# Four quarter operations in place of one for the low part of each weight tile, on GpSimd

## The reference, cut to what matters

```python
x = x + 0.5 * SwiGLU(rmsnorm(x))                      # ffn1, inner width 2816
P = rmsnorm(x) @ w_in                                 # attention q/k/v | RWKV | gates
A = dilated attention, three groups of windows        # 8 heads of 64
R = RWKV-7 time mixing                                # 8 heads of 64
x = x + (sigmoid(gA) * (A @ w_branch_attn) + sigmoid(gR) * (R @ w_branch_rwkv)) @ w_out
x = x + 0.5 * SwiGLU(rmsnorm(x))                      # ffn2
```

## Time and profile before

| | us |
|---|---|
| median of 3 runs | 1869.22 |
| lowest and highest | 1863.80 and 1869.26 |
| the profiled execution's own time | 1864.62 |
| its span, first to last instruction | 1862.8 |
| mean granted TensorE clock | 0.982 of full speed |

### The profile page before, as it was taken

The page is one execution under the profiler, slowest core; times in us unless marked ns, Lnnn a source line. Parts: engine busy times, 40 slices in busy tenths (PEclk is TensorE's granted clock), DMA queues, the critical chain, the costliest instruction groups (busy, mean ns, idle before and its releaser), DMA issues.

```text
span 1862.8 us, 41273 instructions
## 1 busy us (share of the span) xinstructions
PE 1767.9 (95%) x17052; PEld 1680.8 (90%) x17052; DVE 763.9 (41%) x1110; ACT 610.5 (33%) x809; POOL 537.8 (29%) x210
## 2 busy tenths in 40 slices
PE   6999999997989999989999999999989999999999
PEld 5999999996879898987787989897889999999999
DVE  4333023323564645454475463627367333023320
ACT  4332122222423232332243443435224333123321
POOL 2333333442212121111122222223133434333332
PEclk9999999998999999999899999999999999999999
DMA  4334233332432234221154444435433333333343
GB/s 162 113 124 133 101 113 124 121 120 78 179 133 81 90 109 146 80 88 59 37 197 174 162 172 165 176 140 213 177 118 115 113 124 129 125 101 124 125 138 121
DMA packets 53111, 237.48 MB, mean 127 GB/s; under 512 B 7040, under 2 KB 7680, under 8 KB 51584
## 3 DMA queue, kind: packets, MB, share of 16 engines
q1 hardware_dynamic: 45120, 219.40, 34.2%
q10 hardware_dynamic: 7872, 16.37, 2.3%
HBM read 217.98 MB, written 71.76 MB: 156 GB/s over the span
## 4 chain that ended last, share of the span: by engine, by line
PE 55%; issue 24%; DVE 11%; POOL 5%; ACT 2%; DVEq 1%; ACTq 1%; POOLq 0%; PEldq 0%; DMA 0%; PEld 0%
PE ps L343 41%; POOL w_lo L330 5%; PE ps L789 3%; DVE qkv L1988 2%; DVE work L379 1%; DVE work L380 1%; PE ps L1847 1%; DVE qkv L1094 1%; ACT w_hi L325 1%; PE ps L1785 1%; DVEq L2039 1%; PE ps L1771 1%; DVE probs L383 0%; DVE xx L1135 0%; DVE qkv L1101 0%
## 5 line engine op out<-in xcount | busy, mean ns | idle before, releaser
L330 POOL TENSOR_TENSOR w_lo<-w_raw,w_hi 128x1024 fp32r<-128x1024 f32 (+1 forms) x202 | 532.0, 2634 | 1305.8 <-ACT w_hi L325 1305.7
L343 PE MATMUL ps<-h_hi,w_hi 128*128 128x288 f32 x2464 | 554.1, 307 | 25.8 <-DVE h_lo L464 11.2
L343 PE MATMUL ps<-h_hi,w_lo 128*128 128x288 f32 x2464 | 528.9, 296 | 0.0
L343 PE MATMUL ps<-h_lo,w_hi 128*128 128x288 f32 x2464 | 528.2, 296 | 0.0
L343 PEld LDWEIGHTS ps<-h_hi,w_hi 128*128 128x128 f32 x2464 | 398.8, 190 | 50.1 <-issue 20.6
L343 PEld LDWEIGHTS ps<-h_lo,w_hi 128*128 128x128 f32 x2464 | 398.3, 189 | 0.0
L343 PEld LDWEIGHTS ps<-h_hi,w_lo 128*128 128x128 f32 x2464 | 398.1, 189 | 0.0
L325 ACT ACTIVATE w_hi<-w_raw 128x1024 fp32r<-128x1024 f32 (+1 forms) x204 | 226.3, 1110 | 461.0 <-PE ps L343 443.9
L343 PE MATMUL ps<-g_hi,w_hi 128*128 128x288 f32 x704 | 151.4, 297 | 0.1
L343 PE MATMUL ps<-g_lo,w_hi 128*128 128x288 f32 x704 | 151.2, 296 | 0.0
L343 PE MATMUL ps<-g_hi,w_lo 128*128 128x288 f32 x704 | 151.2, 296 | 0.0
(11 more groups left out here) (364 smaller groups left out, 1919.4 us busy)
## 6 DMA issues: line engine op xcount, KB each, us to landing
w_raw<-in_w SPq DMA_DIRECT2D x172, 512.0 KB, 3.7
w_raw<-in_w SPq DMA_DIRECT2D x32, 704.0 KB, 4.1
kv<-in_kc SPq DMA_DIRECT2D x32, 576.0 KB, 6.1
kv<-in_vc SPq DMA_DIRECT2D x32, 576.0 KB, 7.6
cache_out<-in_cache SPq DMA_DIRECT2D x28, 576.0 KB
gates<-gate_out ACTq DMA_DIRECT2D x16, 288.0 KB, 2.3
cache_out<-in_cache SPq DMA_DIRECT2D x8, 480.0 KB
kvT<-qkv ACTq DMA_DIRECT2D x4, 864.0 KB, 7.1
```

Of the source, the lines that this page charges most:

```text
L330: nc.gpsimd.tensor_tensor(w_lo[par_][:, 0:words], w_raw[par_][:, 0:words], w_hi[par_][:, 0:words].bitcast(F32), ALU.subtract).then_inc(lo_ ...
L343: last = nc.tensor.matmul(ps[:, b + c, 0:HC], w[par_][:, wk], a[:, k, c * HC:(c + 1) * HC], start=(first and k == 0), stop=(end and k == n ...
```

## The change

`split_lo` issues four subtractions, each on a quarter of the tile's columns (256 of 1024, or 352 of 1408), instead of one. POOL waits once before the first and signals once, after the last. Nothing else is changed.

```diff
         def split_lo(pool, P, par_, words):
             pool.wait_ge(hi_done, 2 * P + par_ + 1)
-            nc.gpsimd.tensor_tensor(w_lo[par_][:, 0:words], w_raw[par_][:, 0:words],
-                                    w_hi[par_][:, 0:words].bitcast(F32), ALU.subtract).then_inc(lo_done, 1)
+            for i in range(4):
+                c = slice(words // 4 * i, words // 4 * (i + 1))
+                last = nc.gpsimd.tensor_tensor(w_lo[par_][:, c], w_raw[par_][:, c], w_hi[par_][:, c].bitcast(F32), ALU.subtract)
+            last.then_inc(lo_done, 1)
```

## The result

The kernel with four quarters takes **1853.41 us** in the median of 6 runs (1847.63 to 1856.85), the kernel before, run beside it, 1867.31 us in the median of its 6 (1863.8 to 1869.26). The ratio is 0.9925, with a 95% interval of 0.9907 to 0.9943. The profiled execution took 1854.38 us, 10.2 less than the one of before.

The account below looks back on a forecast made before the run. PE, busy 95% of the span, was taken as the bound, so gains come only from its 95 us idle. Costs of +4.6 and gains of -11.25 us gave -6.6, off the median: 1862.6 us, range 1856 to 1877.

Parts of the forecast that it names:

- DVE gets in between two pieces: At every quarter, a waiting DVE operation gets its turn after at most 0.6 to 0.7 us; POOL pays about 0.6.
- POOL doesn't let DVE in: Rival: the next quarter takes the inputs first, DVE waits 2.79 us instead of 2.39; up to +11.6 us, 1881; chance 0.20.
- The gains are hidden or given back: Rival: attention and merge gaps end with the next late thing, half the gain comes through; -1.0 us, 1868; chance 0.20.
- A short operation costs more than the line says: Rival: at 0.40 us per added operation, 38 even FFN units and seven tight units pay; +9.3 us, 1878.5; chance 0.10.
- The price, +4.6 us: Four first down units cost +1.6 us, waits at 15.02, 39.40 and 1447.05 +3.0; the 38 even units 0.
- Mix norm, -1.55 us: At 451.73, line 406 waits only for the first quarter, so PE's sum at 454.25 starts earlier: -1.55 us.
- Merge, -4.4 us: At the merge's end, `m_lo` no longer waits for whole low parts; PE starts about 1371.9 instead of 1376.26: -4.4 us.
- FFN2's norm, -0.4 us: Before 1436.30, four DVE operations each wait for a quarter; only 0.4 of PE's 1.31 us is gained.
- Attention, -4.9 us: In four periods line 1988 ends earlier and PE's waits of 0.28, 0.33 and 0.62 go: -4.9 us.
- RWKV, 0: In four periods PE is 1.4 us late for a low part but loses a 1.47 wait: 0, between -3 and +3.
- Idle time as a whole, -6.6 us: Sum of all terms over the kernel, +4.6 - 11.25 = -6.6 us, all from PE's idle time.
- From 1869.2 us: Starting time from which the -6.6 us was taken: the median of three runs of the kernel before, giving 1862.6.

Follow-up runs that it names:

- e3_longer: Kernel before with the low part whole, plus a short POOL operation of 120 columns into a scratch tile that carries the signal: 1875.0 us, ratio 1.0052.
- e4_half: Kernel before with the low part in two halves in every stage: 1853.1 us, ratio 0.9936.
- e5_rw4: Kernel before with quarters only in the mix norm and RWKV stages: 1862.8 us, ratio 0.9985.
- e6_at4: Kernel before with quarters only in the attention stage: 1859.8 us, ratio 0.9966.
- e7_mg4: Kernel before with quarters only in the merge and output projection: 1859.0 us, ratio 0.9966.
- e1_mid4: Kernel before with quarters in mix norm, RWKV, attention, merge and output projection, both FFNs whole: 1849.9 us, ratio 0.9909.
- e2_ffn4: Kernel before with quarters in both FFNs only, everything between them whole: 1871.7 us, ratio 1.0036.
- e10_tight4: Kernel before with quarters only at each FFN half's first two pairs of up units and first pair of down units: 1871.9 us, ratio 1.0050.
- e8_mid2: Kernel before with halves in all stages outside the FFNs, both FFNs whole: 1850.2 us, ratio 0.9919.
- e12_mix244: Kernel before with FFNs whole, halves in mix and RWKV, quarters in attention, merge and output projection: 1849.2 us, ratio 0.9914.
- e11_ffn8: Kernel before with eight pieces per low part in both FFNs, the middle whole: 1881.9 us, ratio 1.0097.

## Why the prediction was right in sign and wrong in size

The mechanism was right, and so was nearly every term in which a wait was read from the trace. Three things failed. The term for RWKV was put at 0, from one period read and multiplied by four; it is -1.8 us. TensorE's clock was put at nothing, without a reason; by the runs it gives about 3 us. And the forecast started from a median of three runs that lay high, 2 us of the 9.2 between forecast and result. The points in turn:

- **DVE gets in between two pieces** (the assumption on which all gains hung). Right. The merge's rows and the RWKV rows show it at seams with no wait and no signal, and e3_longer and e4_half show that it is the seams inside the low part that matter. The forecast's 0.6 to 0.7 us of waiting was too much: DVE operations take 1.12 to 1.18 in place of 0.76, and POOL pays (4.41 - 2.82) / 4 = 0.4 us for each that comes in, where 0.6 was taken.
- **POOL doesn't let DVE in** (slower, chance 0.20). Fell: its own mark, 1.3 against 2 us, is answered by 1118 ns for `m_lo`. The rule of the Trainium skill (GPSIMD Engine Reference, 2.1 Instruction dispatch) that was set beside it, that each of GpSimd's cores goes on with the next instruction when its own share is done, doesn't lead here to a POOL that holds on to its inputs.
- **The gains are hidden or given back** (0.20). Fell: e5 to e7 bring together what e1_mid4 does.
- **A short operation costs more than the line says** (0.10). Fell: 0.43 us for three added operations, 1.00 for seven (2.39 to 3.39 or 3.40), 0.143 each in both. The Trainium skill (GPSIMD Engine Reference, 3.1 Elementwise), from whose figures I had estimated 0.18 for three, doesn't agree with the trace.
- **The price, +4.6 us.** The places were right: four first down units at 0.39 to 0.49, 2.33 to 3.28 and 2.33 to 3.27 at 1447.05 and 39.40, and no wait in the even units. Waits on `w_lo` rise by 4.6 us in e2_ffn4 and in e10_tight4. In time this costs 6.6 and 7.1 us in medians when it stands alone; with the middle split too, the change is by the ratios 3.0 us (0.16%) above e1_mid4, by the medians 3.5, but from another group of runs. Between 3 and 7 the runs don't decide.
- **Mix norm, -1.55 us.** Right: the gap of 4.52 us is 2.90 now.
- **Merge, -4.4 us.** Right as idle time: 7.75 to 3.31. Measured alone (e7_mg4) it brings 5.5 us of idle time and 6.3 by the ratio; 4.4 of the 5.5 are this wait, the rest are waits of under 0.5 us elsewhere.
- **FFN2's norm, -0.4 us.** It is 1.31 to 0.72, so -0.6.
- **Attention, -4.9 us.** The three waits went as said, 1.23 us a period, but by another path: DVE gets ahead at the low part before, and the operation at line 1988 meets none. A period is 1.44 us shorter; the other 0.2 is in PE's busy time. e6_at4 has 6.2 us less idle time.
- **RWKV, 0.** This term failed. It put four waits of 1.4 us on `w_lo` against four of 1.47, from the reading of one period. PE's waits on the feature arrays (`qkv`) in the kernel before were in fact 4.4 us in three periods and 2.0 in the remaining one, the first in time:

```profile
PE ps L754 <- DVE qkv L1101: 4.4, 3, 1.5
...
PE ps L754 <- DVE qkv L1097: 2.0, 1, 2.0
```

  Both are gone from the list after (6.4 us), against three waits of 1.17 and 1.04 more at 519.43 (1.62 to 2.66 in e5_rw4): 4.6. That leaves -1.8 us.
- **Idle time as a whole, -6.6 us.** It is -10.1. Wait by wait in the change's own trace, with the forecast beside it: `w_lo` in the FFNs +4.6 (+4.6), mix norm -1.6 (-1.55), FFN2's norm -0.6 (-0.4), merge -4.4 (-4.4), attention -5.0 (-4.9), RWKV -1.8 (0). Two waits on `h_lo` that no term named, 0.51 us at 24.33 and 0.44 at 469.91, are gone as well; as the first is also missing in e6_at4 and the second in e7_mg4, which leave those stages whole, they are chance. That makes -9.8; the rest is pieces of 0.35 us and less, such as the span's end, where the trace of before has 3.70 us without PE and every other has 3.35. The four stages alone (e5 to e7 and e2) add up to -13.0 of idle time, so terms under 1 us aren't settled by single traces.
- **The clock, never in the sum.** The change ran at a mean clock of 0.9838 in its 6 executions, the kernel before at 0.9816 to 0.9821 in the 45 of the three groups. What 0.002 is worth can be read in two ways. Half speed for a share s of the span lowers the mean clock by s/2 and costs s/2 of the time, so it is at most 3.7 us, and nearer to 2.8, since 16 of the 68.3 us at the lower level in the trace of before fall into PE's gaps. And of the 45 executions of the kernel before, the six at 0.980 took 1868.3 us in the mean and the eight at 0.983 took 1862.9; a line through all 45 falls by 1.6 us for each 0.001, which gives 3.3. So -10.1 and about -3 make -13. Against the 45 executions (medians 1864.8 to 1866.1) the change is 11.4 to 12.7 us faster, against the six run beside it 13.9. With the same line, the sum of idle time and clock gives +10.1 for e3_longer (9.8 in medians), +7.4 for e10_tight4 (7.1) and -12.4 for e4_half (-12.0); for e1_mid4, e8_mid2 and e12_mix244 it is 2 to 3 us off. That the clock adds to the gain is what the sums bear out; why this kernel draws more of it is not shown, and it isn't steady from kernel to kernel: e4_half has 16 us less idle time and a clock of 0.980, and e2_ffn4, e3_longer and e10_tight4, with new gaps, have 0.978 to 0.980.
- **From 1869.2 us.** The difference was taken off a median of three. Six runs gave 1867.31, and the 45 of the three groups have medians of 1864.8 to 1866.1. 2 us of the 9.2 between forecast and result come from there, though not of the gain.

## What to carry to other kernels

Where two engines shut each other out of a resource, one long operation holds up the other engine for its whole length; one or two seams in it (a fixed 0.14 us each, here) give most of that back. Look for the places where the other engine's late result is what the bound engine waits for, split there, and leave the operation whole where the bound engine waits for it itself: here that is halves outside the FFNs. When a sum is made of small terms, read every wait of every period of a loop, not one period times four. A change in the bound engine's gaps may bring or cost another few us by its clock, so compare executions at the same clock. And when a wait moves to another name in the list, look in the timeline whether it is the same gap.

## What the runs showed of the hardware that was not expected

- **Seams need no wait.** A DVE operation that waits for a POOL operation with two inputs goes ahead at the end of a piece even when the next piece is ready (1363.96: 1.11 us among four quarters, where 2.77 had been).
- **The cost of a further GpSimd operation is steady.** 0.143 us each for pieces of 256 and of 128 columns, back to back.
- **A wait of 0.1 us costs 0.2 and leaves no wait behind.** In e11_ffn8 38 units lose 0.2 us each, and the profile books it as busy time of PE. A list of waits that doesn't grow is no proof that nothing waits.
- **A DVE operation that reads one tile is held up too.** Line 2038 in attention takes 2.59 us against a whole low part and 0.49 without.
- **The same 17052 matmuls are 1762.6 to 1778.0 us of busy time.** Most of the difference up to the 1775.2 of e3_longer goes with the granted clock, which is at the lower of its levels for 48 us (e5_rw4, e7_mg4) to 92 us (e3_longer) of one execution, also in stages whose code and idle times didn't change: e2_ffn4 has a stretch of 3.4 us at half speed at 1193, in attention, where the trace of before has none. In e11_ffn8 (1778.0) it is the unlisted waits. So one execution tells a difference of 5 us only if the clock is read with it.
